# Attention by head pairs in row and column halves of TensorE, in a hybrid attention and RWKV-7 layer

## The chip, the cores and the metric

One NeuronCore of a Trainium2 chip runs one launch of the kernel. The metric is the device time of that launch in microseconds (us). A profiled execution gives the span of the work on the core, and its own time lies a little above the span.

## The reference: what is computed

One decoder layer runs on a prompt of 512 tokens and on 8 single decode tokens. The 1024 input features are projected to 3456 columns: 27 tiles of 128. Twelve tiles are q, k and v of 8 attention heads of width 64, fifteen belong to 8 RWKV-7 heads of width 64. The prompt's attention is

```
s = einsum(q_blk, kg) * 64 ** -0.5 - slopes * dist          # three dilation branches
p = exp(s - lse);  out = sum over branches of wts * (p @ vg)
```

The kernel folds the three branches into one additive table per head (`abias`, 128x512): the logarithm of how many branches see a key, less the distance penalty. So each head is a causal softmax over at most 512 keys. RWKV time mixing follows (decay by a low-rank product, normalised keys, a delta-rule state in chunks of 64 tokens), then the output projection, a layer norm, a gated convolutional FFN of width 2816 and a second layer norm.

## The kernel before, in words

The program is written by hand, engine by engine, each with its own in-order list; semaphores tie the lists together. There is no planner. What is said below of lines refers to the kernel before.

**The input projection** (`in_product`) is a loop over 27 slots, one slot for each tile of 128 output columns. `SLOTS` names them: "r" is an RWKV tile, "a" an attention tile (0 to 3 are q, 4 to 7 are k, 8 to 11 are v, each tile holding two heads, one in partitions 0 to 63 and one in 64 to 127). A slot has two halves of 264 columns (528 = 512 prompt tokens and 16 for the decode tokens). A half is 8 blocks of 3 products in a split format (high x high, high x low, low x high), 24 matmuls, into PSUM bank (2s + half) mod 3. After each of the first seven blocks of a half, `beside(half, i)` may put other TensorE work into the stream.

**What each engine does per slot.** SyncE loads the weights two slots ahead (`weights`), ScalarE rounds them (`w_high`) and VectorE takes the rest (`w_low`), both one slot ahead; a slot's products wait for `w_low`. ScalarE empties both halves (`evac`); for an "r" tile VectorE then makes the token shift (`shift`, two passes).

**Attention before** goes by units: one unit is one head and one block of 128 queries, so 32 units; block q has (q + 1) x 128 keys. A unit takes three half slots. `scores` multiplies q and k (contraction of 64, so it lies in one row half of the array), `soft` on VectorE adds the bias table and takes the maximum, `att_exp` on ScalarE exponentiates and sums, `scale` on VectorE divides, `probs_t` transposes on TensorE through bank 4, `pt_copy` on ScalarE takes the result out, and `values` multiplies with v into a column half of bank 5. A table `ticks` starts one unit per half slot in four runs of eight: from slot 4, 11, 16 and 21. Scores use bank 3; `sw` and `pt` have two buffers each.

**RWKV preparation** is threaded through the same slots: `low_rank` in slots 2 to 5, one product pair per half slot with its sigmoid on ScalarE; `key_in`, `key_square`, `decay_sums` in slots 4 to 9; the key norm in slots 9 to 12; `decays` and `transform` (five VectorE passes) in slots 12, 17, 22 and 24. In VectorE's list `transform` stands ahead of the attention work of its slot, and each half slot's attention work stands behind what precedes it there.

After the 27 slots come the RWKV chunks with the decode attention beside them, the output projection and the FFN. The change touches none of that code, but it sets when `mix_lo` of the last two heads is done, for which the first copies of the next stage wait.

Of the kernel before, what the change touches and what calls it, by code (L numbers as in the profile page):

```python
# [14 lines left out]
P = 128  # L15
# [4 lines left out]
H = 8  # L20
# [50 lines left out]
UNITS = TB * H  # L71
CH = 64
# [76 lines left out]
def layer(nc, a):  # L149
# [68 lines left out]
    tmp = sb(pa, "tmp", [P, XC])  # L218
# [3 lines left out]
    sw = sb(pa, "sw", [P, 2, T])  # L222
    pt = sb(pa, "pt", [P, 2, T])
    vtok = sb(pa, "vtok", [P, TB, AW])
# [224 lines left out]
    ticks = {}  # L449
    for c, first in enumerate((4, 11, 16, 21)):  # L450
        for i in range(H):
            ticks[first + i // 2, i % 2] = H * c + i
    ticks[25, 0], ticks[25, 1], ticks[26, 0] = UNITS, UNITS + 1, UNITS + 2
# [37 lines left out]
    def _(sp):  # L491
# [10 lines left out]
        def bias(h):  # L502

            if h >= 2:
                sp.wait_ge(a_biased, TB * (h - 1))
            sp.dma_start(abias[:, h % 2, :], a["abias"][h]).then_inc(b_landed[h % 2], 16)
# [231 lines left out]
    def _(ac):  # L738
# [61 lines left out]
        def att_exp(u):  # L800
            n = (u % TB + 1) * P
            ac.wait_ge(a_max, u + 1)
            ac.activation(sw[:, u % 2, 0:n], sw[:, u % 2, 0:n], ACT.Exp, bias=nmax[:, u:u + 1],
                          accum_out=rsum[:, u:u + 1]).then_inc(a_exp, 1)
            own(a_exp)

        def pt_copy(u):
            n = (u % TB + 1) * P
            ac.wait_ge(a_probs_t, u + 1)
            if u >= 2:  # L810
                ac.wait_ge(a_pv, u - 1)
            ac.activation(pt[:, u % 2, 0:n], banks[:, 4, 0:n], ACT.Copy).then_inc(a_pt, 1)
            own(a_pt)

        def att_mix(c):
            ac.wait_ge(a_pv, H * (c + 1))
# [3 lines left out]
        def att_tick(k):  # L820
            if 2 <= k < UNITS + 2:
                pt_copy(k - 2)
            if k < UNITS:
                att_exp(k)
            if k >= 3 and (k - 3) % H == H - 1:
                att_mix((k - 3) // H)

        def low_sigmoid(g):
            c, i = divmod(g, 2)
            dst, bias = ((yy, C_W0), (aa, C_A0))[i]  # L830
            ac.wait_ge(lora_ps, g + 1)
            ac.activation(dst[:, c, :].rearrange("p (a b) -> p a b", a=2), banks[:, 6:8, 0:XH], ACT.Sigmoid,
                          bias=col(bias + c)).then_inc(lora_out, 1)
            own(lora_out)
# [18 lines left out]
        for s in range(N_IN + 1):  # L853
# [8 lines left out]
            if s - 1 in v_slots:  # L862
                v_tok_copy(v_slots.index(s - 1))
            if s in (12, 17, 22, 24):
                decays((12, 17, 22, 24).index(s))
            for half in range(2):
                if 2 <= s < 2 + CC:
                    low_sigmoid(2 * (s - 2) + half)
                if (s, half) in ticks:
                    att_tick(ticks[s, half])  # L870
                if half == 1 and 5 <= s < 5 + CC:
# [1682 lines left out]
```

## Time and profile before

| | us |
|---|---|
| median of 3 runs (lowest, highest) | 973.67 (972.17, 975.32) |
| time of the profiled execution | 975.93 |
| its span | 974.1 |
| busy: TensorE matmul, weight load | 891.2, 820.4 |
| busy: VectorE, ScalarE, GpSimd | 516.7, 333.2, 259.2 |
| mean granted TensorE clock | 0.96 |

The page's slices show a TensorE that is 90% busy or more in nearly every slice, with dips in the first third. Matmuls overlap in the array and their ends are modelled, so a busy TensorE says only that a matmul was in it; how long a matmul costs is read from the distance between two starts. By granted clock 1.00 is 2.4 GHz and 0.50 is 1.2 GHz. The first matmul of slot 2 starts at 24.07 us and the last slot ends at 283.70 us.

### The profile page before, as it was taken

How to read it: one execution, taken by the hardware profiler on the slowest of the kernel's cores; microseconds unless marked ns; L12 is line 12 of the kernel's file. 1: busy time of each engine (PE TensorE's matmuls, PEld its weight loads, DVE VectorE, ACT ScalarE, POOL GpSimd, SP SyncE). 2: the span in 40 equal slices, each digit the busy share in tenths (PEclk: the TensorE clock that was granted, in tenths of full speed). 3: DMA queues.
4: the chain of work that ended last, by engine and by line, in shares of the span. 5: the costliest groups of instructions: out<-in, count | busy, mean ns of one | idle time of the engine just before them, and what ended most of it. 6: DMA issues, size and time to landing. Idle time of an engine off the chain costs nothing.

```text
span 974.1 us, 22370 instructions
## 1 busy us (share of the span) xinstructions
PE 891.2 (91%) x9660; PEld 820.4 (84%) x9660; DVE 516.7 (53%) x758; ACT 333.2 (34%) x551; POOL 259.2 (27%) x111
## 2 busy tenths in 40 slices
PE   5988989998989688798999879999999999999995
PEld 5867978787777677677998779999999999999994
DVE  4247674545656757762464446776666665000026
ACT  4464433434331202123232644433333333211124
POOL 0000000000014360801252524543444344343410
PEclk9999999999999879999999879999999999999997
DMA  7201302124126332433012203233223322323302
GB/s 255 69 23 65 98 23 86 45 69 151 33 72 157 94 88 79 121 112 133 24 49 75 65 24 108 91 107 106 89 87 88 94 100 79 100 80 94 102 2 89
DMA packets 31299, 83.42 MB, mean 86 GB/s; under 512 B 5128, under 2 KB 8392, under 8 KB 30688
## 3 DMA queue, kind: packets, MB, share of 16 engines
q1 hardware_dynamic: 30048, 79.82, 26.6%
q10 hardware_dynamic: 1152, 2.16, 0.6%
q8 instruction: 76, 1.25, 0.5%
q14 instruction: 23, 0.19, 0.1%
HBM read 75.87 MB, written 5.91 MB: 84 GB/s over the span
## 4 chain that ended last, share of the span: by engine, by line
PE 77%; DVE 14%; ACT 4%; issue 3%; DMA 1%; POOL 1%; ACTq 0%; DVEq 0%; POOLq 0%
PE banks L1733 76%; DVE rw L1161 2%; DVE xx L1161 1%; DVE ms L1161 1%; DVE w_lo L1161 1%; DVE pm L1161 1%; DMA att<-in_x 1%; ACT x_hi L1069 1%; ACT z L1072 1%; DVE carry L1161 1%; PE banks L1777 1%; DVE rw L1164 1%; DVE z L1161 1%; DVE z L1164 1%; DVE sw L1164 1%
## 5 line engine op out<-in xcount | busy, mean ns | idle before, releaser
L1733 PE MATMUL banks<-x_hi,w_hi 128*128 128x264 f32 (+1 forms) x784 | 215.5, 308 | 16.3 <-DVE x_lo L1161 13.6
L1733 PE MATMUL banks<-x_hi,w_lo 128*128 128x264 f32 (+1 forms) x784 | 201.3, 290 | 0.0
L1733 PE MATMUL banks<-x_lo,w_hi 128*128 128x264 f32 (+1 forms) x784 | 201.2, 290 | 0.0
L1733 PEld LDWEIGHTS banks<-x_hi,w_hi 128*128 128x128 f32 x784 | 141.6, 195 | 41.5 <-issue 26.5
L1733 PEld LDWEIGHTS banks<-x_lo,w_hi 128*128 128x128 f32 x784 | 142.4, 196 | 0.1
L648 POOL TENSOR_TENSOR w_lo<-w_raw,w_hi 128x1024 fp32r<-128x1024 f32 (+1 forms) x40 | 95.6, 2389 | 176.0 <-ACT w_hi L761 175.8
L1733 PEld LDWEIGHTS banks<-x_hi,w_lo 128*128 128x128 f32 x784 | 142.0, 195 | 0.0
L648 POOL TENSOR_TENSOR wx_lo<-w_raw,wx_hi 128x1024 fp32r<-128x1024 f32 (+1 forms) x36 | 86.1, 2392 | 100.7 <-ACT wx_hi L761 100.2
L656 POOL MEMSET kv<- 32x4608 f32 x1 | 3.9, 3938 | 282.5 <-PE banks L1733 282.5
L1164 DVE SCALAR_TENSOR_TENSOR z<-z,banks 128x260 f32<-128x260 f32 (+1 forms) x24 | 12.4, 516 | 122.5 <-PE banks L1733 115.3
L1733 PE MATMUL banks<-x_hi,wx_hi 128*128 128x260 f32 x352 | 73.6, 283 | 0.0
L1733 PE MATMUL banks<-x_hi,wx_lo 128*128 128x260 f32 x352 | 73.6, 283 | 0.0
L1733 PE MATMUL banks<-x_lo,wx_hi 128*128 128x260 f32 x352 | 73.4, 283 | 0.0
L1164 DVE SCALAR_TENSOR_TENSOR cv<-gp,par,cv 128x544 f32<-128x544 f32 x44 | 68.3, 1553 | 1.6
L1161 DVE TENSOR_TENSOR h_lo<-hh,h_hi 128x520 fp32r<-128x520 f32 x22 | 51.5, 2339 | 23.8 <-ACT h_hi L1106 23.8
L1161 DVE TENSOR_TENSOR w_lo<-w_raw,w_hi 128x1024 fp32r<-128x1024 f32 x27 | 33.1, 1225 | 52.2 <-ACT w_hi L744 51.8
L761 ACT ACTIVATE w_hi<-w_raw 128x1024 fp32r<-128x1024 f32 (+1 forms) x40 | 41.6, 1039 | 45.6 <-PE banks L1733 44.6
L1733 PEld LDWEIGHTS banks<-x_hi,wx_hi 128*128 128x128 f32 x352 | 55.4, 188 | 0.2
L1733 PEld LDWEIGHTS banks<-x_hi,wx_lo 128*128 128x128 f32 x352 | 55.4, 188 | 0.0
L1733 PEld LDWEIGHTS banks<-x_lo,wx_hi 128*128 128x128 f32 x352 | 55.2, 188 | 0.0
L761 ACT ACTIVATE wx_hi<-w_raw 128x1024 fp32r<-128x1024 f32 (+1 forms) x36 | 37.3, 1037 | 46.3 <-PE banks L1733 45.0
L1100 ACT ACTIVATE act<-cv 128x512 f32<-128x512 f32 x22 | 13.9, 632 | 94.9 <-DVE cv L1164 94.9
(256 smaller groups left out, 1934.2 us busy)
## 6 DMA issues: line engine op xcount, KB each, us to landing
w_raw<-in_w SPq DMA_DIRECT2D x87, 512.0 KB, 3.5
w_raw<-in_w SPq DMA_DIRECT2D x16, 448.0 KB, 3.3
kv<-in_ck SPq DMA_DIRECT2D x16, 192.0 KB, 3.6
kv<-in_cv SPq DMA_DIRECT2D x16, 192.0 KB, 3.1
att<-in_x ACTq DMA_DIRECT2D x8, 264.0 KB, 7.4
att_out<-att SPq DMA_DIRECT2D x1, 2112.0 KB, 9.2
z<-in_xc SPq DMA_DIRECT2D x1, 2080.0 KB, 7.6
y_out<-z SPq DMA_DIRECT2D x8, 260.0 KB, 2.2
```

The costliest lines, as they stand in the source:

```text
L648: pool.tensor_tensor(lo[:, 0:n * P], w_raw[:, s % 2, 0:n * P], hi[:, 0:n * P].bitcast(F32), ALU.subtract)\
L656: pool.memset(kv[96:P, :], 0.0).then_inc(kv_zero, 1)
L761: ac.activation(w_at(l)[0][:, 0:n * P], w_raw[:, s % 2, 0:n * P], ACT.Copy).then_inc(w_hi_ready, 1)
L1069: ac.activation(x1_hi[:, c, span(half)], z[:, c, span(half)], ACT.Identity, bias=col(C_L1B + c))\
L1072: ac.activation(z[:, c, span(half)], z[:, c, span(half)], ACT.Identity, bias=col(C_L1B + c)).then_inc(ln_z, 1)
L1100: ac.activation(act[:, 0:T], cv[:, 0:T], ACT.Silu).then_inc(act_ready, 1)
L1161: return ve.tensor_tensor(out, a0, a1, op)
L1164: return ve.scalar_tensor_tensor(out, a0, s, a1, op0, op1)
L1733: return pe.matmul(out, l, r, start=start, stop=stop)
L1777: ins = pe.transpose(banks[:, 4, j * P:(j + 1) * P], sw[:, u % 2, j * P:(j + 1) * P], ident[:, :])
```

## The change

Attention goes by pairs of heads. `scores(k)` issues the products of both heads of a tile behind each other, head p in row half p of the array and into bank 6 + p. `values(k)` alternates between the two heads, head p in column half p of the array, both in bank 5. A pair is one tick, so there are 16 ticks instead of 32 units, each tick a whole slot: scores in block 2 of the first half of slot 10 + k, the two transposes in blocks 5 and 6 of the first half of the next slot (banks 4 and 3), values in block 3 of its second half. `sw` has four buffers; `tmp` becomes a view of `pt`.

`SLOTS` is reordered: the four key tiles of RWKV come first (slots 1 to 4), the four value tiles last (21 to 24). `low_rank(c)` issues both low-rank products of a tile at once, one per row half, in slots 2 and 3 (two per slot). `key_in`, `key_square` run in slots 2 to 5, the sums in 3 to 6, the key norm in 7 to 9 with two alternating bank pairs. `transform` moves to slots 10, 14, 18, 22 and, in VectorE's list, behind the attention work of its slot. Bias tables are loaded two at a time ahead of the weights of slots 16, 20 and 24, when all the ticks of the pair before have used theirs. `att_mix` and `mix_lo` of the last tile move behind the last slot.

The core of the diff:

```
-SLOTS = [("r", 0), ("a", 0), ("a", 4), ("a", 8), ("r", J_KS), ("r", J_KS + 1), ("r", J_KS + 2), ("r", J_KS + 3),
-         ("a", 1), ("a", 5), ("a", 9), ("r", J_RS), ("r", J_VS), ("a", 2), ("a", 6), ("a", 10),
-         ("r", J_RS + 1), ("r", J_VS + 1), ("a", 3), ("a", 7), ("a", 11), ("r", J_RS + 2), ("r", J_VS + 2),
-         ("r", J_RS + 3), ("r", J_VS + 3), ("r", 1), ("r", 2)]
+SLOTS = [("r", 0), ("r", J_KS), ("r", J_KS + 1), ("r", J_KS + 2), ("r", J_KS + 3), ("a", 0), ("a", 4), ("a", 8),
+         ("r", J_RS), ("a", 1), ("a", 5), ("a", 9), ("r", J_RS + 1), ("a", 2), ("a", 6), ("a", 10), ("r", J_RS + 2),
+         ("a", 3), ("a", 7), ("a", 11), ("r", J_RS + 3), ("r", J_VS), ("r", J_VS + 1), ("r", J_VS + 2), ("r", J_VS + 3),
+         ("r", 1), ("r", 2)]
...
+TICKS = UNITS // 2
+S_TICK = 10
+S_SHAPE = [S_TICK + TB * c for c in range(CC)]
+S_VTOK = [10, 12, 16, 20]
...
-        late = {10: 2, 11: 3, 16: 4, 18: 5, 21: 6, 23: 7}
         for s in range(2, N_IN):
+            if s in (16, 20, 24):
+                bias(s // 2 - 6)
+                bias(s // 2 - 5)
             weights(s)
-            if s in late:
-                bias(late[s])
-            if s == 9:
-                sp.wait_ge(lora_ps, 2 * CC)
+            if s == 6:
+                sp.wait_ge(lora_ps, CC)
                 sp.dma_start(low_up[:], a["bsel"]).then_inc(bsel_landed, 16)
...
+            if s >= S_TICK + TB + 1 and (s - S_TICK - 1) % TB == 0:
+                att_mix((s - S_TICK - 1) // TB - 1)
+            if s in S_VTOK:
+                v_tok_copy(S_VTOK.index(s))
+            if s in S_SHAPE:
+                decays(S_SHAPE.index(s))
+            if s in (2, 3):
+                low_sigmoid(2 * (s - 2))
+            if s == 7:
+                ac.wait_ge(kk_cl, 1)
+                ac.activation(knorm[:, :], knorm[:, :], ACT.Sqrt).then_inc(n_root, 1)
+                own(n_root)
+            k = s - S_TICK
+            if 1 <= k <= TICKS:
+                pt_copy(2 * k - 2)
+                pt_copy(2 * k - 1)
+            if s < N_IN:
+                evac(s, 0)
+            if s in (2, 3):
+                low_sigmoid(2 * (s - 2) + 1)
+            if 2 <= s < 2 + CC:
+                key_square(s - 2)
+            if 0 <= k < TICKS:
+                att_exp(2 * k)
+                att_exp(2 * k + 1)
...
+            if s >= S_TICK + TB + 1 and (s - S_TICK - 1) % TB == 0:
+                mix_lo((s - S_TICK - 1) // TB - 1)
+            if 2 <= s < 2 + CC:
+                key_in(s - 2)
+            if 3 <= s < 3 + CC:
+                decay_sums(s - 3)
+            if s == 7:
+                ve.wait_ge(n_sum, CC)
+                ve.tensor_scalar(knorm[:, :], banks[:, 5, 0:SUM], 1e-24, None, ALU.max).then_inc(kk_cl, 1)
+                own(kk_cl)
+                ve.wait_ge(n_root, 1)
+                link(ve.reciprocal(knorm[:, :], knorm[:, :]))
+                tt(kbig[:, :].rearrange("p (g t) -> p g t", g=4), knorm[:, :].unsqueeze(1).broadcast_to([P, 4, SUM]),
+                   par[:, C_QUAD:C_QUAD + 4].unsqueeze(2).broadcast_to([P, 4, SUM]), ALU.mult).then_inc(n_inv, 1)
+                own(n_inv)
+                ve.wait_ge(lora_out, 2 * CC)
+                ve.tensor_copy(gath[:, :, 1, :], yy[:, :, T + 1:XC:2]).then_inc(ga_done, 1)
+                own(ga_done)
+            if s in (8, 9):
+                key_norm(2 * (s - 8))
+                key_norm(2 * (s - 8) + 1)
+            k = s - S_TICK
+            if 0 <= k < TICKS:
+                for p in range(2):
+                    soft(2 * k + p)
+                for p in range(2):
+                    scale(2 * k + p)
+            if s in S_SHAPE:
+                transform(S_SHAPE.index(s))
...
+        def scores(k):
+            c, q = divmod(k, TB)
+            n = (q + 1) * P
+            if k == 0:
+                pe.wait_ge(kk_ap, CC)
+            else:
+                pe.wait_ge(a_biased, 2 * k)
+            for p in range(2):
+                ins = mm(banks[:, 6 + p, 0:n], att[half_rows(p), c, q * P:q * P + P], att[half_rows(p), CC + c, 0:n])
+            ins.then_inc(a_scores, 1)
...
+        def values(k):
+            c, q = divmod(k, TB)
+            pe.wait_ge(a_pt, 2 * k + 2)
+            if q == 0 and c >= 1:
+                pe.wait_ge(a_mix_hi, c)
+                pe.wait_ge(a_mix_lo, c)
             for j in range(q + 1):
-                ins = mm(banks[lo:lo + 64, 5, q * P:(q + 1) * P], vtok[:, j, h * HD:(h + 1) * HD],
-                         pt[:, u % 2, j * P:(j + 1) * P], j == 0, j == q)
+                for p in range(2):
+                    h = 2 * c + p
+                    ins = mm(banks[half_rows(p), 5, q * P:(q + 1) * P], vtok[:, j, h * HD:(h + 1) * HD],
+                             pt[:, p, j * P:(j + 1) * P], j == 0, j == q)
             ins.then_inc(a_pv, 1)
...
-        def low_rank(g):
-            c, i = divmod(g, 2)
-            if g == 0:
+        def low_rank(c):
+            if c == 0:
                 pe.wait_ge(const_landed, 16 * N_CONST)
                 pe.wait_ge(lo_act, 1)
             else:
-                pe.wait_ge(lora_out, g)
+                pe.wait_ge(lora_out, 2 * c)
             for half in range(2):
-                ins = mm(banks[:, 6 + half, 0:XH], low_up[64 * i:64 * i + 64, c * P:(c + 1) * P],
-                         rw[64 * i:64 * i + 64, J_WA, half * XH:(half + 1) * XH])
+                for i, b in enumerate((6, 3)):
+                    ins = mm(banks[:, b + half, 0:XH], low_up[half_rows(i), c * P:(c + 1) * P],
+                             rw[half_rows(i), J_WA, half * XH:(half + 1) * XH])
             ins.then_inc(lora_ps, 1)
...
-                if (half, i) == (0, 0) and s - 1 in v_slots:
-                    v_tokens(v_slots.index(s - 1))
-                k = ticks.get((s, half))
-                if k is not None:
-                    if i == 1 and k < UNITS:
+                k = s - S_TICK
+                if half == 0:
+                    if i == 0 and s in S_VTOK:
+                        v_tokens(S_VTOK.index(s))
+                    if i == 2 and 0 <= k < TICKS:
                         scores(k)
-                    if i == 3 and 2 <= k < UNITS + 2:
-                        probs_t(k - 2)
-                    if i == 5 and k >= 3:
-                        values(k - 3)
-                if i == 6 and 2 <= s < 2 + CC:
+                    if i in (5, 6) and 1 <= k <= TICKS:
+                        probs_t(k - 1, i - 5)
+                    if i == 6 and 3 <= s < 3 + CC:
+                        key_sums(s - 3)
+                if (half, i) == (1, 3) and 1 <= k <= TICKS:
+                    values(k - 1)
+                if i == 6 and s in (2, 3):
                     low_rank(2 * (s - 2) + half)
-                if (half, i) == (0, 6) and 6 <= s < 6 + CC:
-                    key_sums(s - 6)
-                if i == 6 and (s, half) in ((10, 0), (10, 1), (11, 0), (11, 1)):
-                    key_spread(2 * (s - 10) + half)
+                if (s, half, i) in ((8, 0, 6), (8, 1, 1), (9, 0, 1), (9, 0, 5)):
+                    key_spread(((8, 0, 6), (8, 1, 1), (9, 0, 1), (9, 0, 5)).index((s, half, i)))
```

## Rows read from the trace of the kernel before

**Rows 1.** Windows, slots 2 to 26: length; busy PE, PEld, DVE, ACT, POOL; clock, DMA.

```profile
24.07:283.70 259.63, 240.70 (x1602) 202.95 (x1600) 140.78 (x250) 111.60 (x210) 0.38 (x1) 0.97 0.21 67
```

**Rows 2.** Windows, TensorE alone, of ten single half slots: length, busy, clock, DMA.

```profile
166.26:169.19 2.93, 2.93 (x27) 1.00 0.27 95
192.45:197.07 4.62, 4.62 (x35) 1.00 0.00 0
248.32:253.49 5.17, 5.17 (x38) 1.00 0.43 146
229.57:234.85 5.28, 5.28 (x38) 1.00 0.20 20
208.13:213.06 4.93, 4.93 (x32) 1.00 0.14 58
234.85:243.68 8.83, 6.54 (x33) 0.81 0.73 292
169.19:174.65 5.46, 5.29 (x39) 1.00 0.46 145
28.28:32.48 4.20, 4.20 (x30) 1.00 0.37 117
94.02:97.49 3.47, 3.47 (x35) 1.00 0.00 0
106.82:110.64 3.82, 3.82 (x31) 1.00 0.00 1
```

**Rows 3.** Timeline of TensorE: start, length of each group; scores and values.

```profile
206.26 1.09 PE L1733 MATMUL banks<-pt,vtok 128*64 128x128 f32 x8
207.28 0.39 PE L1733 MATMUL banks<-x_hi,w_hi 128*128 128x264 f32 x1
...
208.95 1.12 PE L1733 MATMUL banks<-att 64*128 64x512 f32 x2
210.00 0.39 PE L1733 MATMUL banks<-x_hi,w_hi 128*128 128x264 f32 x1
...
211.87 0.43 PE L1733 MATMUL banks<-pt,vtok 128*64 128x128 f32 x2
212.23 0.39 PE L1733 MATMUL banks<-x_hi,w_hi 128*128 128x264 f32 x1
```

**Rows 4.** Timeline of TensorE: column quarters, then quadrants of the array.

```profile
103.06 0.43 PE L1733 MATMUL banks<-ksq,ksel 128*32 128x132 f32 x8
103.43 0.39 PE L1733 MATMUL banks<-x_hi,w_hi 128*128 128x264 f32 x1
...
284.26 0.45 PE L1733 MATMUL banks<-rw,aa 64*64 64x128 f32 x8
284.53 0.40 PE L1733 MATMUL banks<-rw 64*64 64x128 f32 x8
284.75 0.40 PE L1733 MATMUL banks<-rw,aa 64*64 64x128 f32 x8
```

**Rows 5.** Waits of TensorE up to 290 us: total, times, longest.

```profile
PE banks L1733 <- DVE sw L1164: 17.1, 9, 3.1
```

**Rows 6.** Timeline of VectorE in slot 22.

```profile
230.31 0.71 DVE L1161 TENSOR_TENSOR rw<-pre 128x528 f32<-128x528 f32 x1 [1.96 <-ACT pre L791]
231.85 1.22 DVE L1161 TENSOR_TENSOR w_lo<-w_raw,w_hi 128x1024 fp32r<-128x1024 f32 x1
233.11 0.77 DVE L1164 SCALAR_TENSOR_TENSOR yy<-rw,par 128x528 f32<-128x528 f32 x1
...
236.82 0.16 DVE L1210 RECIPROCAL rinv<-rsum 128x1 f32<-128x1 f32 x1
```

**Rows 7.** Groups by shape, 24 to 284 us, DVE and ACT: busy, mean ns; idle before.

```profile
L1164 DVE SCALAR_TENSOR_TENSOR sw<-banks,abias 128x512 f32<-128x512 f32 x8 | 5.5, 692 | 5.9 <-PE banks L1777 5.7
...
L803 ACT ACTIVATE sw<-sw,nmax 128x512 f32<-128x512 f32 x8 | 5.8, 724 | 12.8 <-DVE nmax L1204 12.8
```

**Rows 8.** DMA issues of the page: kind, count, KB each, us from issue to landing.

```profile
w_raw<-in_w SPq DMA_DIRECT2D x87, 512.0 KB, 3.5
```

More of the change, by code:

```diff
@@ L221, in layer @@
     abias = sb(pa, "abias", [P, 2, T])
-    sw = sb(pa, "sw", [P, 2, T])
+    sw = sb(pa, "sw", [P, 4, T])
     pt = sb(pa, "pt", [P, 2, T])
+    tmp = pt[:, :, :].rearrange("p a t -> p (a t)")[:, 0:XC]
     vtok = sb(pa, "vtok", [P, TB, AW])
@@ L448, in layer @@
     N_CONST = 9
[L449 to L453, printed above, removed]
     v_slots = [S_OF["a", 2 * CC + c] for c in range(CC)]
@@ L861, in _ @@
                 own(lo_act)
[L862 to L871, printed above, removed]
-                    key_square(s - 5)
-                if (s, half) == (9, 1):
-                    ac.wait_ge(kk_cl, 1)
-                    ac.activation(knorm[:, :], knorm[:, :], ACT.Sqrt).then_inc(n_root, 1)
-                    own(n_root)
-                if half == 0 and s < N_IN:
-                    evac(s, 0)
+            if s >= S_TICK + TB + 1 and (s - S_TICK - 1) % TB == 0:
[23 more added lines that the diff above has]
+                att_exp(2 * k + 1)
         def rows_copy(i):
@@ L1217, in mix_lo @@
             own(a_mix_lo)
-        def att_tick(k):
-            if 1 <= k < UNITS + 1:
-                scale(k - 1)
-            if k < UNITS:
-                soft(k)
-            if k >= 3 and (k - 3) % H == H - 1:
-                mix_lo((k - 3) // H)
         def key_in(c):
@@ L1270, in _ @@
                 w_low(s + 1)
-            if 5 <= s < 5 + CC:
-                key_in(s - 5)
-            if s in (12, 17, 22, 24):
-                transform((12, 17, 22, 24).index(s))
-            for half in range(2):
-                if (s, half) in ticks:
-                    att_tick(ticks[s, half])
-                if half == 0 and 4 <= s < 4 + CC:
-                    decay_sums(s - 4)
-                if (s, half) == (8, 0):
-                    ve.wait_ge(lora_out, 2 * CC)
-                    ve.tensor_copy(gath[:, :, 1, :], yy[:, :, T + 1:XC:2]).then_inc(ga_done, 1)
-                    own(ga_done)
-                if (s, half) == (9, 1):
-                    ve.wait_ge(n_sum, CC)
-                    ve.tensor_scalar(knorm[:, :], banks[:, 6, 0:SUM], 1e-24, None, ALU.max).then_inc(kk_cl, 1)
-                    own(kk_cl)
-                    ve.wait_ge(n_root, 1)
-                    link(ve.reciprocal(knorm[:, :], knorm[:, :]))
-                    tt(kbig[:, :].rearrange("p (g t) -> p g t", g=4), knorm[:, :].unsqueeze(1).broadcast_to([P, 4, SUM]),
-                       par[:, C_QUAD:C_QUAD + 4].unsqueeze(2).broadcast_to([P, 4, SUM]), ALU.mult).then_inc(n_inv, 1)
-                    own(n_inv)
-                if (s, half) in ((10, 1), (11, 0), (11, 1), (12, 0)):
-                    key_norm(((10, 1), (11, 0), (11, 1), (12, 0)).index((s, half)))
@@ new lines, in probs_t @@
+        def probs_t(k, p):
+            u = 2 * k + p
+            pe.wait_ge(a_norm, u + 1)
+            if p == 0:
+                pe.wait_ge(v_tok, sum(v <= S_TICK + 1 + k for v in S_VTOK))
+            if k >= 1:
+                pe.wait_ge(a_pt, u - 1)
+            for j in range(k % TB + 1):
+                ins = pe.transpose(banks[:, 4 - p, j * P:(j + 1) * P], sw[:, u % 4, j * P:(j + 1) * P], ident[:, :])
+            ins.then_inc(a_probs_t, 1)
+        def values(k):
[4 more added lines that the diff above has]
+                pe.wait_ge(a_mix_lo, c)
```

103 lines of the change are left out of this document (40 added, 63 removed).

## The prediction

> **What bounds the kernel now.** I read the windows by stage first, then single half slots of the input projection, then the waits of TensorE, then VectorE's timeline in one slot. The change acts on slots 2 to 26. They take 259.63 us of the 974.1 us span, TensorE busy in 240.7 of them, VectorE in 140.8, ScalarE in 111.6 [rows 1]. So TensorE's list sets the time, but it does more than its products need. A half slot with nothing beside it takes 2.93 us at full clock (1.00, which is 2.4 GHz) (the first of [rows 2]). The 25 slots hold 50 halves: 50 x 2.93 = 146.5 us. What is put between the blocks comes on top, each taken from an undisturbed half less 2.93 [rows 2]:
>
> - attention, four kinds of half (scores of block 0, 1, 2, 3, each with the transposes and values of earlier units): 4.62 + 5.17 + 5.28 + 4.93 = 20.00, less 11.72, is 8.28 us per head, 66.2 us for 8 heads;
> - low-rank products 4.20 - 2.93 = 1.27, eight times: 10.2;
> - key sums 0.54, four times: 2.2; key spread 0.89, four times: 3.6;
> - transposes of v: 5.46 - 4.62 = 0.84, four times: 3.4.
>
> Together 232.1 us. The other 27.5 of the 259.63 are stalls. The waits name them: TensorE stood 17.1 us, in 9 places, for VectorE's `sw` [rows 5]. The remaining 10.4 us I put down to the clock behind such waits: the half that starts at 234.85 takes 8.83 us where its undisturbed like takes 4.93, and its granted clock is 0.81, a mixture of 2.4 and 1.2 GHz [rows 2]. A stall so costs 3.9 us.
>
> VectorE's timeline shows the reason. In slot 22 it makes the shift (230.31 to 231.85), `w_low` (to 233.11), all of `transform` (to 236.82, 3.71 us) and only then the attention work for which TensorE's next scores wait [rows 6]. It is not short of time over the stage (140.8 of 259.6), it does things in the wrong order.
>
> **What the pairing takes off TensorE.** The price of a group from the starts [rows 3]: eight records, which are four value products of 128 columns, hold the stream for 1.02 us, one product (two records) for 0.36. So a product of 128 columns costs 0.22 and a group some 0.15 beside. The scores of block 3, 512 columns, cost 1.05, which is 4 x 0.22 and 0.18. By the same step blocks 0 to 2 cost 0.40, 0.61, 0.83, sum of a head 2.89 for scores; values 0.36 + 0.58 + 0.80 + 1.01 = 2.75. A low-rank group (two products of 264 columns) comes to 0.90 + 0.18 = 1.08 this way, but its half is 1.27 longer, so the blocks at both ends of a group give 0.2 more. Hence scores 2.89 + 4 x 0.2 = 3.69 per head, values 3.55, and of the 8.28 there remain 1.04 for the transposes.
>
> After the change scores and values are issued once for two heads, transposes still for each. If the two products run together in their halves of the array, a head pair costs 3.69 + 3.55 + 2 x 1.04 = 9.32, four pairs 37.3, against 66.2: 28.9 us less. `low_rank` goes from eight groups to four: 5.1 less. Together 34.0.
>
> Whether they run together the trace of before doesn't show for these two shapes (64 rows x 128 columns, 128 rows x 64 columns). The bounds: nothing overlaps and only the ends of 36 groups fall away (16 scores, 16 values, 4 low-rank, 36 x 0.2 = 7.2 us), or all does (34.0). More than that is excluded, since a product can't take less than its own columns. The nearest rows lie at the upper end: in the RWKV stage four products in the four quadrants of the array start 0.22 us apart, the price of one [rows 4]; and the key sums, four products of 132 columns in column quarters, take 0.37 where four in a row would need 0.88 [rows 4]. The first quadrant group takes 0.27, 0.05 to 0.06 longer than the next, so I charge 0.06 for each of the 36 groups: 2.2. I take 34.0 - 2.2 = 31.8 us.
>
> The Trainium skill speaks against the column halves: "TensorE: Matmul & The Clock Gate", Part 3, says that a weight load overlaps a running matmul only if its row group differs, and the two value products share all rows. Its table gives 2.38 times for three column tiles; taken as the same efficiency for two (1.59 times) for all the pairs, an estimate by that page is 6.8 us less saving where I charge 2.2, so 920 instead of 915.5. The trace disagrees at least with the first sentence: four products on the same rows in 0.37 us.
>
> **What the new order does to the stalls.** Slot lengths after: 5.86, plus scores of its tick, plus transposes (0.1 per block and head) and values of the tick before. Block 3: 5.86 + 1.25 + 0.6 + 1.0 = 8.7 us. Block 0: 5.86 + 0.6 + 0.8 + 1.2 = 8.5. Block 1: 7.5; block 2: 8.1.
>
> VectorE in the longest slot (block 3, "r" tile before it), from the slot's start: it begins when ScalarE has emptied the last half, about 0.5; shift 1.54 and `w_low` 1.26 [rows 6] to 3.3; two bias passes and two maxima, each at most 0.69 and a gap [rows 7], to 6.2; ScalarE's second exponential, 0.72 [rows 7] and some 0.2 to read the sum, to 7.2; the last division (0.16 [rows 6] and a pass of at most 0.69) to 8.1. TensorE wants the result in block 5 of the next slot, at 8.7 + 2.9. That is 3 us to spare, and VectorE is through within the slot. `w_low` is needed at 8.7 and done at 3.3.
>
> In the slots of `transform` (10, 14, 18, 22) the attention passes are short (block 0), but the divisions wait for exponentials that stand behind two `pt_copy` in ScalarE's list, so they end near 7.1; 3.71 for `transform` gives 10.8 against a slot of 8.5, a lag of 2.3 us. The next slot begins with `w_low`, to 3.6, then `mix_lo` to 4.3; the values of that slot, which wait for it, come at 5.4. In slot 23 a shift stands ahead (slot 22 is an "r" tile): 5.85, a stall of 0.45. The lag is gone one or two slots later.
>
> Slots 2 to 9, RWKV alone: VectorE has shift 1.54, `w_low` 1.26, one pass for `key_in` (at most 0.77) and `decay_sums` (four long passes and two tiny ones, at most 3.7), 7.3 us against slots of 5.86 + 0.54 = 6.4, for three slots running. A lag of 0.9 per slot, 2.7 in all, is less than the 3 us between `w_low` and the next slot's start. `low_rank(1)` waits for two sigmoid passes of 0.7 started when `low_rank(0)` ends: 1.1 + 1.4 is inside the 2.93 of a half. The tightest is the last key norm, for which slot 10's v transposes and first scores wait: by the same count it is there 0.4 us ahead. What hides all this is the projection; if the cover is gone, each miss costs up to 3.9.
>
> SyncE: the two bias tables now stand ahead of `weights(16)` (and 20, 24) and wait for the second bias pass of slot 13, near 5.5 us in it. Tables and weights are one queue, and 512 KB land 3.5 us after issue [rows 8]; two tables and the weights are in within some 8 us, so by the middle of slot 14. The table is wanted 2.9 us into slot 14, that is 6 us after its issue, the weights not before slot 15. I cost this at nothing; a late table would be one stall of 3.9, three times at most.
>
> So stalls of 27.5 become 0.45. **Behind the stage** the last `mix_lo` now stands between the last shift and the copies that the RWKV stage starts from: one pass, 0.7 us later; the decode rows wait for it too, which can make it 1.5. I take 0.7.
>
> **The sum.** 31.8 + 27.5 - 0.45 - 0.7 = 58.1 us. The profiled execution took 975.93 (span 974.1), so 917.8 for it; it stood 2.3 above the median of the runs, and against 973.67 it is 915.5. The rest of the kernel is the same list, shifted. Base work in the stage is then about 200 us; VectorE's 140.8 are 70% of it.
>
> **Rivals.**
>
> 1. The halves of the array don't overlap for these shapes. None does: 7.2 instead of 31.8, 940.1 us. Only the row halves (scores, low rank) don't: 4 x 2.89 and 4 x 0.90 come back, less their stagger, about 14 us: 929.5. Against it stand the quadrants [rows 4].
>
> 2. The softmax chain stays the bound in some slots: the tables late, `transform`'s lag, or the key norm. With one stall of 3.9 in each of four slots 15.6 us come back, 931. For it speaks that a pair needs twice VectorE's and ScalarE's work in one slot, and that the lag after `transform` is 2.3 us. The Trainium skill has this as a rule ("TensorEngine Tiling (Array Packing)", PSUM Bottleneck): with the array tiled, emptying PSUM may become the bound. Against it are the 3 us to spare.
>
> 3. Slower than before: all 16 ticks stall. Attention has one slot per tick where a unit had three halves, and a tick which comes late makes the next late. If the chain from scores to the last division took more than 8.7 + 2.9 = 11.6 us, TensorE would wait in each slot and run on at half clock, 3.9 each, 62.4 in all: 977.9, 0.4% slower. The chain as counted takes 8.1.
>
> **Chances.** Forecast (908 to 922) 0.57; rival 1 0.17 (0.10 with row halves alone); rival 2 0.23; rival 3 0.03. The range holds the forecast and most of rivals 1 and 2: 908 to 938. Its low end is full overlap with no stagger, no loss behind the stage (912.6) and some 4 us for clock or stall that I have put into the products. 0.3% is 2.9 us, what a measurement tells from nothing. All cases but the last are faster: 0.96, within 0.3% 0.01, slower 0.03.
>
> **What would show it.** In the profile after, slot 2 starts at 24.07 again and the stage ends near 225. Right for the pairing: the scores of block 3, now four records, hold the stream for 1.1 us and not 1.9; the values of block 3, 16 records, 1.1 and not 1.9. Right for the order: TensorE's waits for `sw` nearly gone, granted clock 1.00 in slots 10 to 26, and starts of slots 8.7, 8.5, 7.5, 8.1 us apart. Wrong: new waits of TensorE for `kk`, `low_rank`'s sigmoids, `mixa_lo` or `vtok`, or the RWKV stage longer than before by more than 2 us.

## The result and the profile after

| | before | changed |
|---|---|---|
| median, us | 974.35 | 914.13 (913.14 to 915.60) |
| profiled execution, us | 975.93 | 914.03 |
| its span | 974.1 | 912.2 |
| slots 2 to 26 | 258.97 | 198.38 |
| everything behind slot 26 | 691.06 | 689.91 |
| mean granted clock | 0.96 | 0.97 |

The ratio of the times is 0.9386, 95% interval 0.9365 to 0.9407. The forecast for the profiled execution was 917.8 us, 58.1 less than before; 61.9 were measured. That the median lies closer, 914.13 for 915.5, is partly luck: the forecast took off 2.3 us because the profiled execution of before stood that far above its median, and here it stands 0.1 below. The rows of slots 2 to 26 and of what lies behind them are read from the first matmul of slot 2 to 0.12 us behind the start of the last one of slot 26 (which is 283.04 us before the change; [rows 1] reads to 283.70 and so holds 0.66 us of the next stage's first wait).

Windows of the changed kernel: all slots from 2 on, those from 10 on, and the rest. Columns as in [rows 1]. TensorE's busy time now fills the stage, 197.51 of 198.29 us, at a granted clock of 1.00 (0.97 before), and VectorE's 140.07 us are nearly the 140.78 of before, now 71% of the stage. The rest of the kernel is 1.15 us shorter, which is less than it varies between executions (see the last experiment).

```profile
23.91:222.20 198.29, 197.51 (x1602) 178.44 (x1600) 140.07 (x249) 101.68 (x201) 0.00 (x0) 1.00 0.28 87
...
81.44:222.20 140.76, 139.98 (x1138) 124.86 (x1136) 98.95 (x187) 75.85 (x162) 0.00 (x0) 1.00 0.29 89
222.20:912.20 690.00, 635.21 (x7967) 602.23 (x7965) 367.05 (x492) 211.18 (x327) 258.93 (x106) 0.96 0.28 87
```

Four half slots of the changed kernel, columns as in [rows 2]: the first and second half of slot 25 (scores of block 3; values of block 2), a half with a low-rank group, the second half of slot 23.

```profile
205.59:210.43 4.84, 4.84 (x37) 1.00 0.01 3
210.43:214.35 3.92, 3.92 (x39) 1.00 1.06 240
28.12:32.33 4.21, 4.21 (x34) 1.00 0.36 125
193.68:197.47 3.79, 3.56 (x31) 1.00 0.37 118
```

The first two bring 1.91 and 0.99 us on top of 2.93. The first was forecast as 1.25 for the scores of two heads and 0.6 for the transposes, the second as 1.0 for the values of two heads. The low-rank half is 4.21 us long with both products in it; with one of them it was 4.20 [rows 2]. Slot 23's half is the one stall that the forecast named, 3.79 us where its likes take 3.49. The starts of slots 13, 14, 15 and 16 lie 8.95, 8.76, 8.54 and 7.46 us behind the one before each; 8.1, 8.7, 8.5 and 7.5 were forecast, the first without the transposes of v (0.84) that its slot also holds.

Timeline of TensorE in the changed kernel, values of block 3 and scores of block 3, each with the block that follows. Twice the records of [rows 3] (16 for 8, 4 for 2) take the same time: 1.02 us from start to start for 1.02, and 1.06 for 1.05. That is the pairing, seen directly: the second head's products add next to nothing.

```profile
119.71 1.09 PE L1730 MATMUL banks<-pt,vtok 128*64 128x128 f32 x16
120.73 0.39 PE L1730 MATMUL banks<-x_hi,w_hi 128*128 128x264 f32 x1
...
206.77 1.13 PE L1730 MATMUL banks<-att 64*128 64x512 f32 x4
207.83 0.39 PE L1730 MATMUL banks<-x_hi,w_hi 128*128 128x264 f32 x1
```

The waits of TensorE for VectorE up to 235 us (total, times, longest). Of 17.1 us for `sw` [rows 5] nothing is left; there are 0.2 us for `mixa_lo` in slot 23 and, behind the last slot, 3.1. The first line lies ahead of slot 2 and the third in the next stage.

```profile
PE banks L1730 <- DVE x_lo L1161: 9.6, 1, 9.6
PE banks L1860 <- DVE mixa_lo L1161: 3.1, 1, 3.1
PE banks L1730 <- DVE xx L1161: 1.5, 1, 1.5
PE banks L1730 <- DVE mixa_lo L1161: 0.2, 1, 0.2
```

VectorE's timeline from slot 22 into slot 23, the counterpart of [rows 6]: shift, `w_low`, then the short tick (184.72 to 188.13), then `transform` to 191.84; slot 23, which began at 189.71, gets its shift at 191.88, 2.2 us late (2.3 were forecast), `w_low` and then `mixa_lo`, done at 195.38. TensorE came for it in the middle of that half.

```profile
181.92 0.71 DVE L1161 TENSOR_TENSOR rw<-pre 128x528 f32<-128x528 f32 x1 [1.39 <-ACT pre L790]
...
183.46 1.22 DVE L1161 TENSOR_TENSOR w_lo<-w_raw,w_hi 128x1024 fp32r<-128x1024 f32 x1
184.72 0.29 DVE L1164 SCALAR_TENSOR_TENSOR sw<-banks,abias 128x128 f32<-128x128 f32 x1
...
187.85 0.29 DVE L1210 TENSOR_SCALAR sw<-sw,rinv 128x128 f32<-128x128 f32 x1
188.17 0.77 DVE L1164 SCALAR_TENSOR_TENSOR yy<-rw,par 128x528 f32<-128x528 f32 x1
...
191.88 0.71 DVE L1161 TENSOR_TENSOR rw<-pre 128x528 f32<-128x528 f32 x1
...
193.43 1.23 DVE L1161 TENSOR_TENSOR w_lo<-w_raw,w_hi 128x1024 fp32r<-128x1024 f32 x1
194.69 0.69 DVE L1161 TENSOR_TENSOR mixa_lo<-banks,mixa_hi 128x512 fp32r<-128x512 f32 x1
```

### The profile page after: what moved, and what is told of

Same layout as the page of the kernel before. It is cut to its first block, busy times and chain, and to the rows that moved or that the text cites. A ratio compares the mean times of both kernels' runs of the same rounds, so it can differ in the third digit from the quotient of the medians.

```text
span 912.2 us, 22353 instructions
## 1 busy us (share of the span) xinstructions
PE 846.9 (93%) x9660; PEld 794.6 (87%) x9660; DVE 518.8 (57%) x758; ACT 324.3 (36%) x544; POOL 259.2 (28%) x111
## 3 DMA queue, kind: packets, MB, share of 16 engines
q8 instruction: 76, 1.25, 0.5%
## 4 chain that ended last, share of the span: by engine, by line
PE 84%; DVE 11%; ACT 3%; issue 1%; ACTq 0%; POOL 0%; DVEq 0%; POOLq 0%
PE banks L1730 82%; DVE xx L1161 2%; DVE ms L1161 1%; DVE carry L1161 1%; DVE pm L1161 1%; DVE z L1164 1%; PE banks L1784 1%; DVE sscore L1384 1%; DVE z L1161 1%; DVE rw L1161 1%; DVE x_lo L1161 1%; ACT z L1072 0%; ACT x_hi L1069 0%; ACT z L1132 0%; ACTq L765 0%
## 5 line engine op out<-in xcount | busy, mean ns | idle before, releaser
L1730 PE MATMUL banks<-x_hi,w_hi 128*128 128x264 f32 (+1 forms) x784 | 209.4, 300 | 15.7 <-DVE x_lo L1161 13.4
L1730 PEld LDWEIGHTS banks<-x_lo,w_hi 128*128 128x128 f32 x784 | 140.4, 193 | 0.1
L1164 DVE SCALAR_TENSOR_TENSOR z<-z,banks 128x260 f32<-128x260 f32 (+1 forms) x24 | 12.4, 515 | 122.5 <-PE banks L1730 115.3
L1100 ACT ACTIVATE act<-cv 128x512 f32<-128x512 f32 x22 | 13.9, 632 | 94.3 <-DVE cv L1164 94.2
```

The costliest lines, as they stand in the source:

```text
L1100: ac.activation(act[:, 0:T], cv[:, 0:T], ACT.Silu).then_inc(act_ready, 1)
L1164: return ve.scalar_tensor_tensor(out, a0, s, a1, op0, op1)
L1730: return pe.matmul(out, l, r, start=start, stop=stop)
```

## The experiments

The kernels ran in several sittings, in which the kernel before had medians of 974.35 to 977.16 us, so small differences are read from the stage of the profile (slots 2 to 26) and not from the whole time. The stage repeats to 0.1 us: of the changed kernel it takes 198.38 in two profiles, and of the variant profiled twice 198.23 and 198.19.

### The second head's scores one block later

```
-            for p in range(2):
-                ins = mm(banks[:, 6 + p, 0:n], ...)
-            ins.then_inc(a_scores, 1)
+            ins = mm(banks[:, 6 + p, 0:n], ...)
+            if p == 1: ins.then_inc(a_scores, 1)
...
-                    if i == 2 and 0 <= k < TICKS: scores(k)
+                    if i in (1, 2) and 0 <= k < TICKS: scores(k, i - 1)
```

> The changed kernel, but the score product of the second head stands one block later than that of the first, so that the two never run together; everything else as changed. Theory (the two row halves run together and TensorE's list sets the stage): the price of a score group comes back once per pair, 3.69 us for each of the four tiles, 14.8 us in all, 914.1 + 14.8 = 929. Rival (the gain comes from the order and the stalls, the pairing is worth little because a product in half the rows runs alone anyway): under 4 us.

Measured: 927.75 us, ratio to before 0.9500 (0.9467 to 0.9534). The stage took 212.84 us, 14.5 more than the changed kernel's, where 14.8 were expected. TensorE's timeline shows the two products of one tick, each now with a block behind it and the full price:

```profile
219.62 1.12 PE L1730 MATMUL banks<-att 64*128 64x512 f32 x2
220.67 0.39 PE L1730 MATMUL banks<-x_hi,w_hi 128*128 128x264 f32 x1
...
221.23 1.12 PE L1730 MATMUL banks<-att 64*128 64x512 f32 x2
222.28 0.39 PE L1730 MATMUL banks<-x_hi,w_hi 128*128 128x264 f32 x1
```

So the row halves run together when the two products are neighbours, the second product is then free, and in this stage a microsecond of TensorE is a microsecond of the kernel. (Of the 14.5 us some 3.2, an estimate from 16 groups at the forecast's 0.2 us, are the second interruption of the stream in each tick, and the rest the products themselves.)

### Values of one head, then of the other

```
-            for j in range(q + 1):
-                for p in range(2):
+            for p in range(2):
+                for j in range(q + 1):
```

> The changed kernel, but a value group issues all blocks of the first head and then all of the second; same 160 records, same groups, only not alternating. Theory (a product overlaps only its neighbour in the list, and only if that one lies in the other column half): a group of q + 1 blocks per head then takes 2(q + 1) products less the one overlap at the change of head, so 0, 0.22, 0.44, 0.66 us more for q = 0 to 3, 1.3 per tile, 5.2 in all, 919.3. Rival (TensorE takes products out of turn, so that the order within a group is free): no change, within 1 us. Third (column halves do not overlap at all): no change either, but then the group of block 3 takes 1.9 us in both kernels, not 1.1.

Measured: 917.73 us; stage 201.15, 2.8 more, between the theory's 5.2 and the rival's nothing. The half slots with the values of block 0, 1, 2 and 3 grew by 0.00, 0.01, 0.26 and 0.50 us, where I had 0, 0.22, 0.44, 0.66; that is 3.1 us for four tiles, less the stall of 0.3 in slot 23, which is gone here. The group of block 3, alternating 1.02 us, now takes 1.52:

```profile
120.42 1.58 PE L1730 MATMUL banks<-pt,vtok 128*64 128x128 f32 x16
121.94 0.39 PE L1730 MATMUL banks<-x_hi,w_hi 128*128 128x264 f32 x1
```

The order within a group matters, so TensorE does not pair products freely; but it reaches further than one neighbour: with two blocks per head (A A B B) the order costs nothing, and with four it costs 0.50 us where four products of 0.22, none overlapped, would cost 0.88. That column halves overlap at all is shown; how far back the overlap reaches is known only as these four numbers.

### The kernel before with transform behind the attention work

```
-            if s in (12, 17, 22, 24):
-                transform((12, 17, 22, 24).index(s))
             for half in range(2):
                 ...
+            if s in (12, 17, 22, 24):
+                transform((12, 17, 22, 24).index(s))
```

> The kernel before the change, with one thing altered: VectorE makes transform behind the attention work of both halves of its slot instead of ahead of it (slots 12, 17, 22, 24). Theory (VectorE's order there is what made TensorE stall): the excess of the four halves goes, 3.9 + 2.4 + 3.9 + 3.9 = 14.1 us, so 974.3 - 14 = 960. Rival (a unit per half slot leaves no room for 3.7 us of other work wherever it stands; the stall moves to the next slot): within 4 us of 974.3.

Measured: 975.3 us, ratio 0.9983 (0.9964 to 1.0003), no change. The stage took 256.64 us, 2.3 less than before the change, not 14. The four halves in question are now undisturbed (slot 12's second half 4.93 us, not 8.83), and the halves behind them have taken over: slot 13's second half 11.48 instead of 6.54, slot 18's 7.13 instead of 5.77, slot 23's 8.68 instead of 5.17, slot 25's 5.99 instead of 4.35. VectorE in slots 12 and 13: `transform` ends at 143.72, and only then come the next shift, `w_low` (145.30) and the next two units (147.28, 151.53).

```profile
140.05 0.77 DVE L1164 SCALAR_TENSOR_TENSOR yy<-rw,par 128x528 f32<-128x528 f32 x1
...
143.03 0.69 DVE L1161 TENSOR_TENSOR rw<-rw,ksq 128x512 f32<-128x512 f32 x1
...
145.30 1.22 DVE L1161 TENSOR_TENSOR w_lo<-w_raw,w_hi 128x1024 fp32r<-128x1024 f32 x1
...
147.28 0.29 DVE L1164 SCALAR_TENSOR_TENSOR sw<-banks,abias 128x128 f32<-128x128 f32 x1
...
151.53 0.42 DVE L1164 SCALAR_TENSOR_TENSOR sw<-banks,abias 128x256 f32<-128x256 f32 x1 [2.46 <-PE banks L1777]
```

TensorE waits for `sw` 13.8 us in this kernel (17.1 before), and once, 1.4 us, its transposes wait for a division. So my rival held, and the diagnosis in the prediction was wrong: the other place for `transform` in the same list moves the stalls to the next slots and takes 2.3 us off, not 14.

### The changed kernel with transform ahead

```
             k = s - S_TICK
+            if s in S_SHAPE:
+                transform(S_SHAPE.index(s))
             if 0 <= k < TICKS:
                 ...
-            if s in S_SHAPE:
-                transform(S_SHAPE.index(s))
```

> The changed kernel, with transform moved back ahead of the attention work in VectorE's list of slots 10, 14, 18, 22. Theory (it is the whole slot per tick that absorbs transform, not its place): soft starts 3.7 us later, the last division of a short tick ends about 10.5 us after the slot's start, TensorE asks for it at 8.5 + 2.5 = 11.0; no stall or a small one, 0 to 2 us, 914 to 916. Rival (the place in the list is what counts, as in the kernel before): four stalls of 3.9 us, 929.7.

Measured: 913.92 us; stage 198.76, 0.4 more. One half (slot 11's first) grew, 3.98 to 4.64, and the stall in slot 23 went. The two kernels and these two experiments make a square: the place of `transform` is worth 2.3 us with one unit per half slot and 0.4, the other way, with one pair per slot. So something else in the change removes the stalls. I take it to be the spacing of the ticks, but that is argued and not shown: the change also gives `sw` four buffers for two and does the RWKV preparation ahead of slot 10, where no attention runs, and no run has one of these without the others.

### The kernel before with the first run of units late

```
-    for c, first in enumerate((4, 11, 16, 21)):
+    for c, first in enumerate((7, 11, 16, 21)):
```

> The kernel before the change, with the first run of eight attention units moved from slots 4 to 7 to slots 7 to 10, behind the low-rank products and their sigmoids; the other three runs as they were. Theory (the two longest stalls, 4.2 and 4.9 us in the second halves of slots 5 and 6, come from ScalarE changing its table between sigmoid and exponential, with the exponential chain of a unit behind it): these 9.1 us go and up to 2 come in where the run now meets the key norm; 974.3 - 8 = 966, table loads in the stage down from 10 to 3 to 5. Rival (VectorE's decay sums and key passes make the stalls, and the new place has its own): within 3 us of 974.3.

Measured: 973.28 us, ratio 0.9980 (0.9964 to 0.9997); stage 256.70, 2.3 less. ScalarE's table loads in the stage fell from ten to four:

```profile
L803 ACT ACT_TABLE_LOAD x2 | 2.6, 1283 | 6.8 <-DVE nmax L1204 6.8
L832 ACT ACT_TABLE_LOAD x1 | 1.3, 1283 | 2.1 <-PE banks L1733 2.1
L875 ACT ACT_TABLE_LOAD x1 | 1.3, 1283 | 0.0
```

and the second halves of slots 5 and 6 lost their stalls with their attention (4.21 and 2.93 us for 10.42 and 9.84). But new ones came where the run now stands: halves of 8.66, 6.93 and 7.22 us in slots 8, 10 and 11, and TensorE's waits for `sw` add up to 13.9 us:

```profile
PE banks L1733 <- DVE sw L1164: 13.9, 9, 2.3
```

The stall moves with the units; another 1.3 us TensorE now waits for the key norm. The theory on the two long stalls is not refuted: in the kernel before, ahead of them, VectorE stood idle for 5.42 us (until 55.85) and 6.65 us (until 72.94), waiting for ScalarE's `pre`, which has sigmoids, exponentials and table loads ahead of it in ScalarE's list. But taking them away there gives little.

### More work for VectorE in each tick

```
                 for p in range(2):
                     soft(2 * k + p)
+                for p in range(2):      # 4 in the second kernel
+                    link(tt(kbig[:, 0:T], kbig[:, 0:T], kbig[:, 0:T], ALU.max))
```

> The changed kernel with two more passes of 512 columns (a maximum of a free tile with itself, result unused) in VectorE's list between the maxima and the divisions of each tick, some 1.45 us per tick, 23 us of added work. Theory (TensorE sets the stage and VectorE has about 3 us to spare per tick): the chain ends at 9.6 instead of 8.1 us, before 11.6; only where transform's lag adds up does mix_lo come late. 2 to 6 us more, 916 to 920. Rival (the softmax chain sets the slots): all of it, 23 us more, 937.

> The same with four added passes, some 2.9 us per tick, 46 us of added work. Theory: VectorE's work for four ticks is then about 37.4 us against 33 of TensorE, so VectorE sets the stage, and TensorE runs partly at half clock behind its waits: 18 to 45 us more, 932 to 959; this is the mechanism of the rival that would have made the change slower. Rival (the chain was the bound already): 46 us more or above, 960. Other rival (VectorE is never near): under 5 us.

Measured: 916.62 us and 927.33 us. The windows of slots 2 to 26 in the two kernels (columns as in [rows 1]):

```profile
23.89:222.83 198.94, 197.60 (x1602) 178.50 (x1600) 162.23 (x281) 102.00 (x201) 0.00 (x0) 1.00 0.28 87
```

```profile
24.31:237.25 212.94, 200.02 (x1602) 179.81 (x1600) 184.33 (x313) 101.67 (x201) 0.00 (x0) 0.99 0.26 81
```

With 22 us more of VectorE work the stage is 0.56 us longer; with 44 us more it is 14.6 us longer, VectorE busy 184.33 of 212.94 us. The first was below my 2 to 6, the second below my 18 to 45, so the spare time was somewhat larger than I had counted. (By the whole time the first kernel, 916.62, lies in its range of 916 to 920; it is the stage that doesn't.) In the second kernel TensorE waits mostly where `transform`'s lag and `mix_lo` meet, in slots 15, 19 and 23, and 1.9 us for a division in slot 26:

```profile
PE banks L1732 <- DVE mixa_lo L1161: 8.0, 3, 4.7
PE banks L1786 <- DVE sw L1210: 1.9, 1, 1.9
```

So the edge of the cover lies between 1.4 and 2.8 us of added work per tick. In the second kernel the last division of an ordinary block 3 tick ends 12.5 us after its slot's start, against 8.1 in the changed kernel, so past the 11.6 at which TensorE asks for the first transposes; the first half of the slot behind grew by 0.35 us for it (4.76 for 4.41). Just behind the edge a late division costs tenths of a microsecond and not 3.9; some 9 of the 14.6 us come at `mixa_lo` (the second halves of slots 15 and 19 grew by 1.7 each, that of slot 23 by 5.9).

### The last mix ahead of the last evacuation

```
+            if s == N_IN: att_mix(CC - 1)      # ScalarE; VectorE: mix_lo(CC - 1)
             if s >= 1:
                 evac(s - 1, 1)                 # VectorE: shift(s - 1)
...
```

> The changed kernel, but behind the last slot ScalarE makes mixa_hi of the last tile ahead of emptying the last half, and VectorE mixa_lo ahead of the last shift. Theory (TensorE's wait of 3.1 us for mixa_lo and the half clock behind it cost the start of the next stage): TensorE starts the decode transposes some 2.5 us earlier, and VectorE's list is 0.7 us shorter behind the last half; 1 to 2 us less, 912.1 to 913.1. Rival (the next stage is bound by other chains and takes it back): no change, within 0.5 us.

Measured: 914.81 us, no change; behind slot 26 its profile has 690.67 us. TensorE at the seam, first in the changed kernel, then here:

```profile
225.53 1.01 PE L1860 MATMUL banks<-ident,att 128*8 128x128 f32 x4 [3.07 <-DVE mixa_lo L1161]
226.47 0.70 PE L1730 MATMUL banks<-rw,aa 64*64 64x128 f32 x8
226.95 0.65 PE L1730 MATMUL banks<-rw 64*64 64x128 f32 x8
...
231.15 0.68 PE L1730 MATMUL banks<-level,xx 64*64 64x64 f32 x16
```

```profile
223.03 0.60 PE L1864 MATMUL banks<-ident,att 128*8 128x128 f32 x4 [0.53 <-ACT pre L790]
223.56 0.45 PE L1734 MATMUL banks<-rw,aa 64*64 64x128 f32 x8
223.83 0.40 PE L1734 MATMUL banks<-rw 64*64 64x128 f32 x8
...
226.61 0.60 PE L1873 MATMUL banks<-ident,rw 128*128 128x128 f32 x4
229.89 1.12 PE L1734 MATMUL banks<-level,xx 64*64 64x64 f32 x16 [2.68 <-DVE xx L1163]
```

The wait of 3.1 us for `mixa_lo` is gone and TensorE begins at 223.03 instead of 225.53. But it is then through with this work before VectorE is, and stands from 227.2 to 229.89. In the changed kernel the groups at 226.47 and 226.95 lie 0.48 apart (0.27 here): half clock, on work that nothing urgent follows, and by 231.15 the products of the inverse run at full clock, 0.68 us for 16 records. Here those take 1.12 us, at half clock. The early start is paid back behind the next idle stretch: the first products of the next step start at 237.37 us, in the changed kernel at 236.64, and in its second profile at 236.15. This is one profile of the variant against two; what happens behind 237 us is not followed.

### Fewer interruptions

```
-                    if i == 2 and 0 <= k < TICKS: scores(k)
                     if i in (5, 6) and 1 <= k <= TICKS: probs_t(k - 1, i - 5)
+                    if i == 6 and 0 <= k < TICKS: scores(k)      # second kernel: all three at i == 5
```

> The changed kernel, with a tick's scores moved from block 2 to block 6 of the first half, directly behind the second transposes. Theory (a group that follows another saves the 0.1 to 0.2 us that the split blocks lose at its start, and the softmax chain has 3 us to spare): scores 1.5 us later, chain through at 9.5 of 11.6 us, no stall, 16 x 0.15 = 2.4 us less in the stage, 911.7. Rival (the later start makes the divisions or transform late): up to 4 stalls of 3.9, above 914.

> As the one before, but both transposes and the scores stand together behind block 5 of the first half, one interruption instead of three. Theory: some 0.1 us more saved per tick than there, 3 to 4 us less than the changed kernel in the stage, 910.5. Rival: the second transposes wait for the second division without a block between them and TensorE stalls; above 914.

Measured: 915.48 and 912.45 us; stages 198.13 and 198.23, against 198.38. So the chain did have the room, as the theory says, and the gain of 2 to 4 us didn't come; the 0.2 us that did are no more than the stall in slot 23, 3.79 us in the changed kernel and 3.48 and 3.50 here. The 0.2 us around a group don't belong to the interruption of the stream as such. The trace of the second kernel shows where they went, in slot 25, both transposes and the scores in a row:

```profile
207.58 0.82 PE L1784 MATMUL banks<-ident,sw 128*128 128x128 f32 x6
208.32 1.13 PE L1730 MATMUL banks<-att 64*128 64x512 f32 x4
```

The six transposes hold the stream for 0.74 us until the scores start; in the changed kernel, three and three, they hold it for 0.25 and 0.24. So the 0.2 us now stand inside the group, ahead of the scores: they come with the step from one kind of product to the other, wherever it lies. What in that step takes them is not shown. The 912.45 lies in the work behind the stage (688.1 us in its profile), whose code is untouched. To see whether it stays I ran the changed kernel and this one side by side.

> The changed kernel once more, unaltered, beside the next one on the same chip. It gives the size by which the work behind the projection differs between executions of the same code: 690 us in one profile of it, 688 to 694 in the profiles of the variants, whose code is the same there. 914, with some 690 to 692 behind slot 26.

> The variant with both transposes and the scores in one interruption once more. Its stage took 198.2 us like the changed kernel's 198.4, yet its time was 912.5. If the gain is real it comes from the work behind the stage and stays: 912.5, 1.5 us below the run beside it. If it is the spread of that work, the two medians agree within 1 us.

Measured: 916.19 (ratio to before 0.9388, 0.9363 to 0.9413) and 914.78 us (0.9364, 0.9339 to 0.9391), stages 198.38 and 198.19, the work behind them 690.95 and 693.08. Twice the median was below the changed kernel's, by 1.7 and 1.4 us, but the intervals overlap and the profile shows nothing that would make it; in this last pair the profiled rest was longer, not shorter. I leave it open and don't call it a faster version. The spread of that part, 688 to 694 us over the fourteen profiles of this study, is larger than anything these two kernels could differ by.

## Why the prediction was right, and where not

The forecast was right in its size and in what the change does; its reason for the stalls before the change was wrong.

**Undisturbed sum and stalls.** The count of TensorE's own work before (232.1 us, 27.5 of stalls) was sound: with the stalls away and each pair at the price of one group the same terms give 198.1, with the one stall 198.6, and the stage took 198.4. Only 0.66 us of the 27.5 belonged to the first wait of the next stage; the stalls were 26.9. The measured 61.9 us are 34.0 + 26.9 - 0.3 in the stage (60.6), 1.15 behind it and 0.16 ahead of slot 2.

**The pairing, 34.0 less 2.2.** It gave all 34.0. The 0.06 us that I charged for each of 36 groups is at most 0.01: the scores of block 3 take 1.06 for 1.05, values 1.02 for 1.02. This is the one term of the stage that was mis-sized by more than a microsecond, by 2.2 less some tenths. The estimate by the Trainium skill ("TensorE: Matmul & The Clock Gate", Part 3), 920 us, came out too high; its sentence that a weight load overlaps only across row groups is not what these column halves do, eight products on the same rows in 1.02 us, the time of four. Had I taken the quadrants at their word [rows 4], 913.3 would have stood there.

**The stalls, 27.5 to 0.45.** The number came out (0.3 in slot 23, some tenths for v), and the place too, at 2.2 us of lag. The reason that I gave for the old stalls did not. I wrote that VectorE "does things in the wrong order". The order alone is worth 2.3 us in the kernel before. All nine waits for `sw` there are of one kind: a unit's scores wait for the bias pass of the unit before, and none of the transposes waits for a division. In slot 22 the bias pass stands in VectorE's list behind `transform` and a division:

```profile
237.41 0.56 DVE L1164 SCALAR_TENSOR_TENSOR sw<-banks,abias 128x384 f32<-128x384 f32 x1
238.02 1.18 PE L1733 MATMUL banks<-att 64*128 64x512 f32 x2 [2.29 <-DVE sw L1164]
```

The scores of the unit before start at 230.40, TensorE asks for the next ones at 235.73, 5.3 us later, and waits 2.29 us; the other 1.6 of the 3.9 us come behind it, at a granted clock of 0.81 over the half [rows 2]. Several microseconds of other work on VectorE between two bias passes do not fit in 5.3 us, and the two places tried for `transform` both left it between two. With a pair per slot, scores follow scores after 8.1 to 8.8 us (slots 12 to 22), and the measured chain has room at both ends: in slot 21, a block 3 tick, the bias passes end 5.7 us after the slot's start where the next scores come at 9.9, and the divisions end at 7.3 and 8.1 where the transposes start at 11.6 and 12.4. Forecast were 8.1 and 11.6, so 4.3 us are to spare, not 3, and VectorE may do 22 us of extra work for 0.56. The walk through the new slots was right because it counted the chain against the time until TensorE asks; the same walk through an old slot would have shown this before any run.

One thing I overlooked. With two `sw` buffers a bias pass also waits until the transposes of the unit two before have read its buffer. The passes over 256 keys show it most, 11.2 us in all, those over 512 keys another 5.7 [rows 7]; in the changed kernel, with four buffers, each kind is idle for 0.3 us in all. The row of before:

```profile
L1164 DVE SCALAR_TENSOR_TENSOR sw<-banks,abias 128x256 f32<-128x256 f32 x8 | 3.4, 425 | 11.3 <-PE banks L1777 11.2
```

None of the nine bias passes that TensorE stood for had itself just waited so, but no run has the old spacing with four buffers, so their share in the 26.9 us is open.

**Behind the stage, 0.7 more.** It was 1.2 less. I had the decode rows wait for the last `mixa_lo` and allowed up to 1.5 us for it; TensorE now starts 3.2 us behind the last slot where it started 0.7 us behind it before, 2.5 more, since evacuation, mix, shift and `mix_lo` stand one behind the other there. That the span did not grow for it fits the timelines of the run with the mix ahead: the half clock falls on work with slack. In the spread of that part, 688 to 694 us, neither 0.7 nor 1.2 can be told.

**Rivals.** The first is refuted by the start distances and by the 14.5 us of the first experiment. The second, at 0.23, was too likely: the spare time is there and more. The third overpriced a late tick: with 2.8 us of work added per tick the chain of the block 3 ticks passed its 11.6 us, and TensorE lost 0.35 us behind each, not 3.9. A chain that is late by much more in all 16 ticks was not run.

## What to carry to other kernels

Two products with 64 rows or 64 columns each, in different halves of the array and next to each other in the list, cost here what one costs (1.06 us for 1.05, 1.02 for 1.02); look for such neighbours wherever heads of width 64 meet a 128-wide array. Where a softmax chain over three engines runs beside a stream of matmuls, compare the chain's length with the time until TensorE asks for its result, not the engines' busy shares. Do that for each link: here TensorE stood still at the first one, the scores that need the bias pass, and not at the last. Each of two reorderings at the old distance took 2.3 us out; the change, which widened the distance from some 5 us to more than 8 and brought four buffers and an RWKV preparation out of the way with it, took 27. And a stall that lies at a piece of work need not be caused by its place: move it in the old kernel before believing so.

## What the runs showed of the hardware that was not expected

- Two heads' products in column halves need not alternate one by one: with two blocks per head the order A A B B took no longer than A B A B (3.72 us for the half in both), with three blocks 0.26 us more, with four 0.50.
- The 0.2 us that TensorE's stream of 264-column products loses around a group of another kind didn't fall when three groups were put behind each other: 198.2 us against 198.4, with 32 interruptions less. It moved in between the groups (six transposes 0.74 us ahead of scores, twice 0.25 when apart).
- Taking a wait of 3.1 us away at the start of a stage gave nothing: an idle time of 2.68 us came later instead, with the half clock behind it, 1.12 us for a group of 16 records instead of 0.68.
